# Hybrid decoder trunk on one core: order of the prologue's loads, place of a reciprocal, and the spread of the norms' columns

## The reference, cut to what matters

```
mod = silu(c) @ ada_w[l] + ada_b[l]          # 1024 x 6144: six rows sh1, sc1, g1, sh2, sc2, g2
h = rmsnorm(x, norm1_g[l]) * (1 + sc1) + sh1
proj = h @ w_in[l]                           # split among three head groups
  A) Mamba-2 SSD: conv, chunked scan of 8 blocks of 128 tokens, gated norm
  B) latent attention: rmsnorm of q latents (256) and kv latents (128), up-projections, causal attention
  C) sliding-window attention, window 128, with sinks
x = x + g1 * (concat(A, B, C) @ w_out[l])
h = rmsnorm(x, norm2_g[l]) * (1 + sc2) + sh2
x = x + g2 * ((silu(a) * b) @ ffn_w_down[l]) # a, b: causal conv of width 3 over h @ ffn_w_up[l]
```

## Time and profile before

| | us |
|---|---|
| three runs | 2371.20, 2375.56, 2380.42 |
| median | 2375.56 |
| profiled execution, its own time | 2377.14 |
| its span, first to last instruction | 2375.4 |
| PE busy | 2301.6 (97%) |
| DVE busy | 1636.5 (69%) |
| ACT busy | 1100.5 (46%) |
| POOL busy | 1014.6 (43%) |
| DMA queue of SP | 307.94 MB, 40.3% |

### The profile page before, as it was taken

One profiled execution on the slowest core, in us unless ns is written; L12 is line 12 of the kernel. 1 busy time (PEld: TensorE's weight loads), 2 busy tenths in 40 slices (PEclk: granted clock), 3 DMA queues, 4 the chain that ended last, 5 costly groups with the idle time before them and its releaser, 6 DMA issues.

```text
span 2375.4 us, 31321 instructions
## 1 busy us (share of the span) xinstructions
PE 2301.6 (97%) x11557; PEld 1868.7 (79%) x11557; DVE 1636.5 (69%) x2084; ACT 1100.5 (46%) x1808; POOL 1014.6 (43%) x641
## 2 busy tenths in 40 slices
PE   5999999999999999999999999999999999999998
PEld 5787866788788888888878888567878888888887
DVE  5974467628866767777888544774597666677886
ACT  4435547534444444444452454573444444444445
POOL 1211168533887777400002123233469777770000
PEclk6999999999999999999999999999999999999999
DMA  7661314243243323487546322004413333347763
GB/s 262 233 203 36 85 51 134 94 129 98 74 129 89 111 89 111 138 289 252 163 177 204 107 69 70 8 19 139 146 41 119 105 109 111 89 129 252 239 214 115
DMA packets 272534, 310.73 MB, mean 131 GB/s; under 512 B 36872, under 2 KB 191230, under 8 KB 271358
## 3 DMA queue, kind: packets, MB, share of 16 engines
q1 hardware_dynamic: 272094, 307.94, 40.3%
q10 hardware_dynamic: 288, 0.79, 0.2%
HBM read 246.47 MB, written 61.42 MB: 130 GB/s over the span
## 4 chain that ended last, share of the span: by engine, by line
PE 79%; DVE 10%; ACT 3%; issue 2%; POOL 1%; DMA 1%; DVEq 0%; SPq 0%; ACTq 0%; POOLq 0%
PE bank L1490 30%; PE bank L1505 17%; PE bank L1063 15%; PE bank L1123 5%; PE bank L1321 2%; DVE nt L2179 2%; PE bank L1353 1%; PE bank L1281 1%; DVE hLo L2133 1%; PE bank L1381 1%; DVE hLo L2119 1%; DVE xT L2127 1%; PE bank L1210 1%; DMA raw<-in_ffn_w_up_dram 1%; PE bank L1132 1%
## 5 line engine op out<-in xcount | busy, mean ns | idle before, releaser
L983 POOL TENSOR_TENSOR wLo<-raw,wHi 128x1024 fp32r<-128x1024 f32 x66 | 161.5, 2448 | 465.9 <-ACT wHi L985 465.9
L1680 POOL TENSOR_TENSOR prodLo<-comb,prodHi 128x512 fp32r<-128x512 f32 x160 | 234.6, 1473 | 123.5 <-ACT prodHi L1025 123.5
L1490 PE MATMUL bank<-tHi,prodHi 128*128 128x512 f32 x640 | 250.6, 392 | 4.5 <-DVE tLo L2488 4.1
L1490 PE MATMUL bank<-tHi,prodLo 128*128 128x512 f32 x640 | 250.5, 391 | 0.0
L1490 PE MATMUL bank<-tLo,prodHi 128*128 128x512 f32 x640 | 250.3, 391 | 0.0
L1505 PE MATMUL bank<-gateHi,downHi 128*128 128x512 f32 x616 | 240.3, 390 | 0.0
L1505 PE MATMUL bank<-gateHi,downLo 128*128 128x512 f32 x616 | 239.7, 389 | 0.0
L1505 PE MATMUL bank<-gateLo,downHi 128*128 128x512 f32 x616 | 239.6, 389 | 0.0
L1025 ACT ACTIVATE prodHi<-comb 128x512 fp32r<-128x512 f32 x160 | 100.5, 632 | 249.5 <-PE bank L1490 230.5
L2433 DVE SCALAR_TENSOR_TENSOR ub<-bank,ffp,ub 128x1023 f32<-128x1023 f32 x88 | 112.8, 1282 | 141.8 <-ACT ub L1941 140.3
L1490 PE MATMUL bank<-hHi,prodHi 128*128 128x512 f32 x480 | 187.1, 390 | 5.3 <-POOL prodLo L1680 2.7
(11 more groups left out here) (392 smaller groups left out, 5435.0 us busy)
## 6 DMA issues: line engine op xcount, KB each, us to landing
raw<-in_ffn_w_up_dram SPq DMA_DIRECT2D x88, 512.0 KB, 4.9
gateRaw<-gateOut SPq DMA_DIRECT2D x154, 256.0 KB, 4.2
adaE<-in_ada_w_dram SPq DMA_DIRECT2D x64, 512.0 KB, 5.8
gateOut<-gateSums SPq DMA_DIRECT2D x22, 1024.0 KB, 5.5
raw<-in_w_in_dram SPq DMA_DIRECT2D x34, 512.0 KB, 4.7
downRaw<-in_ffn_w_down_dram SPq DMA_DIRECT2D x66, 256.0 KB, 3.5
raw<-in_w_out_dram SPq DMA_DIRECT2D x28, 512.0 KB, 4.2
downCols<-in_ffn_w_down_dram SPq DMA_DIRECT2D x24, 512.0 KB, 3.7
```

Of the source, the lines that this page charges most:

```text
L983: eng.tensor_tensor(lo[:], raw[slot][:], fview(hi[:]), ALU.subtract).then_inc(s["split_lo"], 1)
L1490: last = mm(o, w[idx][:, c0], moving(idx, kp, hi), start=kp == 0 and q_ == 0, stop=kp == 3 and q_ == 2)
L1680: pool.tensor_tensor(sLoW[idx][:], product_source(js, idx), fview(sHiW[idx][:]), ALU.subtract).then_inc(s["us_lo"], 1)
```

## The change

Three edits. The spread becomes a PE transpose of the broadcast column, at all five places. In the prologue SP issues modulation weights 12 to 15 before both w_in tiles. DVE's reciprocal stands after tile 9 (i == KT + 1) and no longer after tile 12.

```diff
     def spread(pe, out_, column):
 
-        return pe.matmul(out_, column.to_broadcast([P, P]), ident[:], start=True, stop=True)
+        return pe.transpose(out_, column.to_broadcast([P, P]), ident[:])
...
                 for i in range(8, 2 * KT):
-                    if i in (12, 14):
-                        n = (i - 12) // 2
-                        load_win(sp, w_in[0:1], n, n, s[f"next_loaded{n}"])
                     load_adaw(i)
+                for n in range(AHEAD):
+                    load_win(sp, w_in[0:1], n, n, s[f"next_loaded{n}"])
...
-                    if i == KT + 4:
+                    if i == KT + 1:
                         dve.wait_ge(s["n1_rstd"], 1)
                         dve.reciprocal(rst[:, 0:NB], rst[:, 0:NB]).then_inc(s["n1_rstd"], 1)
```

## The result

| | before | after |
|---|---|---|
| median of 7 runs, us | 2375.56 | 2363.46 |
| lowest, highest | 2371.20, 2380.42 | 2360.85, 2369.49 |
| profiled execution, its own time | 2377.14 | 2360.93 |
| its span | 2375.4 | 2359.2 |

The ratio is 0.9946, with a 95% interval of 0.9937 to 0.9956: 12.1 us less by the medians, where 11.4 was forecast. The profiled execution after is one of the fastest of its seven, that before lies above its median, so the two traces are 16.2 us apart; what of this is the change's has to be taken apart.

The account below looks back on a forecast made before the run. TensorE, busy 97% of the span, was taken to bound the kernel, with a barrier ending the prologue. Gains of 5.3 (prologue) and 6.1 (spreads) make 11.4: 2375.6 - 11.4 = 2364.2 us, range 2361 to 2367.

Parts of the forecast that it names:

- Spreads, 6.1 us: Norm spreads behind the prologue: as transposes, one record instead of two, 6.1 us less, bounds 0 to 6.3.
- the first working, 6.3: Norm spreads in both layers: 3.6 us latent plus 2.7 us other norms, before a deduction for the last record's latency.
- Rival A: All spreads: broadcast transpose no cheaper, still two records; only 3.6 us gained, in the prologue, 2372.0; chance 0.07.
- rival D: Stages behind the spreads, such as the FFN's start: half of the 6.1 is lost, 8.3 us gained, 2367.3; chance 0.10.
- Loads in order, tiles 11 to 13 at 35.7, product 15 done at 42.4: Prologue, modulation tiles ahead of w_in: DVE's chain, ending at 48.07 before, gains 5.7 us.
- The reciprocal costs nothing: Prologue, DVE: 0.20 us placed in an existing wait costs nothing there; PE's wait of 1.22 before its spread goes.
- The barrier: End of the prologue: opens after the later of POOL at 47.1 and DVE at 47.0, against 52.38 before.
- Rival B: Prologue: the w_in tiles become the barrier's last arrival, second landing after 43.5; 8.4 us gained in all, 2367.2; chance 0.22.
- The prologue's size, 5.3 us: Prologue: barrier opens at 47.1 instead of 52.38, gaining 5.3 us; upper end 5.4, lower end 2.3.
- Sum: Whole kernel: 5.3 us in the prologue plus 6.1 at later spreads, 11.4 less, giving 2364.2, 0.48% less.
- Rival C: Eight later spread groups: transposes let the PE clock fall, 12.8 us lost against 11.4, 2377.0; chance 0.04.
- 1.8 us of the prologue's gain to the transposed spread: Prologue, PE: eight transposes take 1.94 us where 16 matmul records took 3.78, 1.8 less.

Follow-up runs that it names:

- the repetition: All three edits run again, against the kernel before on the same chip: 2364.23 against 2376.22 us, ratio 0.9940.

## Why the prediction was right

The forecast was 2364.2, the median 2363.46. By its own steps:

- **Spreads, 6.1 us: right, measured 6.4.** One record for each spread, x64, groups of 1.75 and 0.45. The part that I took off for a last record's latency was not there: latency halves too (0.91 to 0.45), so the first working, 6.3, was the better one. Rival A is out.
- **Nothing swallows it** (rival D): right for the latent spreads, which alone gave 3.8 us of 3.7, and in layer 1. In layer 2 rival D has a case at the place that it named: 0.9 us, as much as norm 2's spreads bring there, is lost at the FFN's start. That is a third of D's price (3 us).
- **Loads in order, tiles 11 to 13 at 35.7, product 15 done at 42.4:** DVE could start them at 36.26 and was done at 43.10; 0.6 and 0.7 late, of which the parameters and tiles before them had already brought about 0.5 (line 617's product started at 31.95 before, 32.49 after).
- **The reciprocal costs nothing:** right. That PE's wait of 1.22 ahead of the spread goes by it: true, but it also goes by the loads' order alone, so the edit is worth nothing here.
- **The barrier.** I had POOL at 47.1 and the DVE chain at 47.0, so the layer at 48.6; POOL ended at 47.61 and the layer started at 49.32. Two steps were missing. The first w_in tile landed at 41.80 and not at 41.1, so POOL was still at its first split (42.93 to 45.28) when the second tile's high part was ready at 44.65; I had the second split start at once. And the two engines touch: DVE's last addition of line 423 does not end until POOL has (0.61 or 0.62 in five traces with the new order, 1.15 and 1.05 in two, each ending 0.03 or 0.04 us behind POOL), which puts POOL's end 1.7 us ahead of the layer and not 1.5. It goes the other way as well: where POOL's first split began 0.4 to 0.6 before DVE's last product had ended, it took 2.60 to 2.78 and not 2.35 (five traces). Rival B named the place rightly, and its price of 3 us was too high. SP did hold the w_in DMAs even longer than it feared, until 25.40 + 14.66 = 40.06, but the second tile landed at 43.59, as forecast (43.6), 3.5 us behind the end of its issue; before that was 5.7 (35.34 to 41.08).
- **The prologue's size, 5.3 us.** The two first traces gave 4.56. The start of the layer varies between executions: 53.88, 54.98, 55.50 and 55.79 in the four traces with the old order, mean 55.04; 49.32, 50.67, 49.54, 50.04 and 49.39 in the five with new order and spread and the split as it was, mean 49.79. The difference of the means is 5.25. Both means are 1.2 later than the numbers that I worked with (53.88 and 48.6), so the gain came out right although neither end did; the trace of before was the earliest of its kind.
- **Sum.** 5.25 + 6.4 = 11.7, or 10.8 without the 0.9 lost in layer 2, against 12.1 by the medians and 12.0 for the repetition; the interval (0.9937 to 0.9956, 10.5 to 15.0 us) holds both. What remains is below what the runs can tell; whether the change has any share in fewer falls of the clock stays open.
- **Rival C** is out: 112 transposes in a row ran at a granted clock of 1.00. The Trainium skill, TensorE: Matmul & The Clock Gate, Part 4 (PE-mode transpose), says that the full clock does not engage for transposes; for the f32 128x128 transposes of this kernel the measurement decides against it.

One thing came out right for a reason that I had only half. I counted 1.8 us of the prologue's gain to the transposed spread. In the old order it is worth nothing (the wait behind it grows by as much), and with the loads in order it is worth only what PE would be later than POOL; the kernel with the loads alone started its layer as early, thanks to a clock that rose in that execution. What it is worth there at 1.2 GHz was not measured by itself.

## What to carry to other kernels

Where PE is the bound, look for f32 matmuls whose one operand is the identity: as transposes they take one record instead of two, and the trace before already shows both prices. When a prologue ends in a barrier, list the end of every chain that leads to it before pricing one edit; here moving the loads brought 5 us, and then DVE's, PE's and POOL's chains ended within a microsecond, where no single further edit showed. Before giving POOL's work to DVE, ask whether the two can run at the same time; here they took turns. And before taking the difference of two traces for the change's, lay them over each other at fixed instructions: a third of the difference here was the clock.

## What the runs showed of the hardware

- DVE and POOL took turns with instructions of two SBUF operands. A DVE product (128x1024) begun while POOL was still at a split ended 1.08 us behind POOL's end (six products in four traces; alone it takes 1.28), and a POOL split begun while a DVE product was at work ended 2.20 to 2.22 behind the product's end (ten splits; alone 2.35). So the "4.48 for two" of the earlier trace rows is a product that waited for POOL until 45.61, and POOL's 3.39 there is a split that waited for the DVE product before. A short DVE addition (128x16) ends 0.03 us behind POOL (0.17 us alone, 0.61 to 1.15 beside POOL). DVE instructions with one SBUF operand, or one in PSUM, were not held up: line 632's addition (one operand in a bank) took 0.16 in the middle of POOL's split (46.64, loads only), the reciprocal 0.20 (43.06, spread only).
- PE's clock rose once in a stretch of one-column products and matmul spreads: in the kernel with the loads alone the last 16 products took 1.84 us instead of 3.57. It is the only one of four traces with matmul spreads there in which PE did not wait between the spread and the products (2.2 to 4.5 us in the other three). With transposes, four of eight traces had no such wait, and the clock rose in none. Whether transposes make it rarer stays open, since the transposes of x bring the clock up in every one of the twelve traces, after 13 to 28 of them.
